# Two transformer blocks on one core: closing an output projection's banks one by one, seven of eight norm operands summed by VectorE, and products of the norm one ahead of the residual sums

## The reference, cut to what matters

```
# first block, layers 0 (gated delta net) and 1 (mLSTM)
hs = hs + keep * rms_norm(mix, norm_w[i, 1])
f = conv_ffn(rms_norm(hs, norm_w[i, 2]), ...)
hs = hs + keep * rms_norm(f, norm_w[i, 3])
# second block, layers 0 (short conv, attention) and 1 (GLA, MLA)
x = layer_norm(ALPHA * x + y, ln_mix_g[layer], ln_mix_b[layer])
x = layer_norm(ALPHA * x + swiglu(...), ln_ffn_g[layer], ln_ffn_b[layer])
```

## Time and profile before

| | |
|---|---|
| median of 3 runs | 1445.23 us (1445.07 to 1447.6) |
| span of the profiled execution | 1443.1 us; the median of the runs is 2.1 us above it, and no other time of that execution is listed |
| TensorE busy | 1423.5 us (99%), 11333 matmuls |
| VectorE busy | 1013.4 us (70%), 1701 instructions |
| ScalarE busy | 779.4 us (54%), 1399 instructions |
| mean granted clock of TensorE | 0.999 of full speed |
| chain that ended last | PE 81%, DVE 12%, issue 3%, ACT 3% |

### The profile page before, as it was taken

The page is one execution under the profiler, slowest core; times in us unless marked ns, Lnnn a source line. Parts: engine busy times, 40 slices in busy tenths (PEclk is TensorE's granted clock), DMA queues, the critical chain, the costliest instruction groups (busy, mean ns, idle before and its releaser), DMA issues.

```text
span 1443.1 us, 31771 instructions
## 1 busy us (share of the span) xinstructions
PE 1423.5 (99%) x11333; PEld 1363.9 (95%) x11333; DVE 1013.4 (70%) x1701; ACT 779.4 (54%) x1399; POOL 294.0 (20%) x348
## 2 busy tenths in 40 slices
PE   9999999999999999999999999999999999999997
PEld 8999888899999999999999999999999989999986
DVE  7884957659876477569888477587664687776645
ACT  6556324556655366466565356464453567654542
POOL 3804002103444000002544000013330012033310
PEclk9999999999999999999999999999999999999999
DMA  7551231244655535344666544546556433565552
GB/s 256 177 175 47 88 101 47 93 142 160 190 175 175 175 119 189 103 146 128 193 189 189 182 134 152 164 146 200 183 168 204 152 116 118 163 217 186 183 180 91
DMA packets 60996, 223.57 MB, mean 155 GB/s; under 512 B 6768, under 2 KB 6896, under 8 KB 60528
## 3 DMA queue, kind: packets, MB, share of 16 engines
q1 hardware_dynamic: 60624, 220.17, 48.1%
q10 hardware_dynamic: 288, 2.23, 0.4%
HBM read 221.32 MB, written 1.05 MB: 154 GB/s over the span
## 4 chain that ended last, share of the span: by engine, by line
PE 81%; DVE 12%; issue 3%; ACT 3%; DVEq 1%; ACTq 0%; POOL 0%; POOLq 0%
PE bank L440 20%; PE bank L441 20%; PE bank L442 20%; DVE wlo L415 3%; PE bank L461 2%; PE bank L1168 2%; PE bank L462 1%; PE bank L468 1%; DVE bank L947 1%; PE bank L3284 1%; PE bank L3285 1%; PE bank L3287 1%; ACT cv L831 1%; DVE cv L839 1%; DVE work L1782 1%
## 5 line engine op out<-in xcount | busy, mean ns | idle before, releaser
L415 DVE TENSOR_TENSOR wlo<-raw,whi 128x1024 fp32r<-128x1024 f32 x397 | 501.4, 1268 | 249.3 <-ACT whi L410 248.8
L410 ACT ACTIVATE whi<-raw 128x1024 fp32r<-128x1024 f32 x397 | 415.1, 1056 | 288.6 <-PE bank L442 240.6
L440 PE MATMUL bank<-xs,whi 128*128 128x258 f32 (+2 forms) x1984 | 569.2, 287 | 0.0
L441 PE MATMUL bank<-xs,whi 128*128 128x258 f32 (+2 forms) x1984 | 563.9, 284 | 0.0
L442 PE MATMUL bank<-xs,wlo 128*128 128x258 f32 (+2 forms) x1984 | 561.6, 283 | 0.0
L440 PEld LDWEIGHTS bank<-xs,whi 128*128 128x128 f32 x1984 | 374.2, 189 | 3.0 <-issue 1.6
L442 PEld LDWEIGHTS bank<-xs,wlo 128*128 128x128 f32 x1984 | 375.0, 189 | 0.0
L441 PEld LDWEIGHTS bank<-xs,whi 128*128 128x128 f32 x1984 | 374.3, 189 | 0.6 <-issue 0.2
L440 PE MATMUL bank<-hf,whi 128*128 (+3 forms) x848 | 241.3, 285 | 2.0 <-DVE cv L839 0.8
L441 PE MATMUL bank<-hf,whi 128*128 (+3 forms) x848 | 240.3, 283 | 0.0
L442 PE MATMUL bank<-hf,wlo 128*128 (+3 forms) x848 | 240.2, 283 | 0.0
(11 more groups left out here) (516 smaller groups left out, 1671.8 us busy)
## 6 DMA issues: line engine op xcount, KB each, us to landing
raw<-stream SPq DMA_DIRECT2D x412, 512.0 KB, 3.7
con<-consts SPq DMA_DIRECT2D x1, 1284.5 KB, 10.5
big<-mla ACTq DMA_DIRECT2D x1, 1152.0 KB, 7.8
hs_sb<-hs SPq DMA_DIRECT2D x2, 544.0 KB, 4.2
work<-last ACTq DMA_DIRECT2D x1, 1024.0 KB, 9.1
y_out<-work SPq DMA_DIRECT2D x4, 256.0 KB, 2.0
par<-params SPq DMA_DIRECT2D x1, 420.0 KB, 7.9
par<-params SPq DMA_DIRECT2D x1, 224.0 KB, 4.8
```

Source lines behind the costliest of these rows:

```text
L410: nc.scalar.activation(whi[:, s, :], raw[:, s, :], ACT.Copy).then_inc(hi_split, 1)
L415: nc.vector.tensor_tensor(wlo[:, s, :], raw[:, s, :], whi[:, s, :].bitcast(F32), ALU.subtract).then_inc(block_split, 1)
L440: nc.tensor.matmul(out_, whi[:, slot, w], hi, start=start, stop=False)
L441: nc.tensor.matmul(out_, whi[:, slot, w], lo, start=False, stop=False)
```

## The change

The last two rows of each output projection in `pe_wide` are taken together: bank by bank, six matmuls each, so that bank m closes 6 matmuls after bank m - 1. The number of matmuls is the same. In `post` joints VectorE adds seven squares, not five, and scales seven banks, sum and scaled copy of a tile taking turns; TensorE sums two operands, not four. The high part of the third block goes from ScalarE to VectorE, behind the scaled copies. Behind the scale, the product of tile m + 1 goes ahead of the residual sum of tile m. In `ln` joints VectorE adds seven tiles, TensorE sums two operands, not six; the third block's high part is made by ScalarE as soon as its slot is free, and its low part in two halves, the first before the mean is subtracted, the second behind the third tile. The loads of ScalarE's table go ahead of the splits of the output projection.

```diff
@@ -455,8 +455,12 @@
                 pe.wait_ge(*S("norm", "act").at(f"{name}_hi{k}"))
                 for j in range(AHEAD):
                     o, s = rhs_out(g0 + j, phase), (b0 + j) % SLOTS
+                    by_half = name.startswith("ln") and j == AHEAD - 1
+                    if k == 0 and by_half:
+                        pe.wait_ge(*S("norm", "dve").at(f"{name}_third"))
+                    if k == (KC // 2 if by_half else 0):
+                        pe.wait_ge(block_split, splits(b0 + j))
                     if k == 0:
-                        pe.wait_ge(block_split, splits(b0 + j))
                         pe.wait_ge(bank_free, g0 + j + 1)
...
+        def last_two():
+
+            pe.wait_ge(block_split, splits(b0 + n - 1))
+            for k in (n - 2, n - 1):
+                ready(pe, k, None)
+            for m in range(8):
+                for k in (n - 2, n - 1):
+                    last = three(rhs_out(g0 + m, phase), (b0 + k) % SLOTS, m, hf[:, half[k], T], hf[:, half[n + k], T], False, k == n - 1)
+                    if m == 7:
+                        last.then_inc(block_used, 1)
+                    elif k == n - 1:
+                        last.then_inc(*S("wide", "pe").mark(f"{phase}_m{m}"))
 
         if n == 22:
             rows(0)
             with pe.Fori(0, 2) as i:
                 for k in range(1, 9):
                     rows(k, i)
-            for k in range(17, 22):
+            for k in range(17, n - 2):
                 rows(k)
+            last_two()
...
-    FIRST_SUM, IN_BANK = 5, 5
+    FIRST_SUM, IN_BANK = 7, 7
...
-        sums_pe(pe, name, post_src(name), g, ((5, True, False), (6, False, False), (0, False, False), (7, False, True)), T1, POST_FIRST[name])
+        sums_pe(pe, name, post_src(name), g, ((0, True, False), (7, False, True)), T1, POST_FIRST[name])
...
-        split_hi(act, used_after(phase) + AHEAD - 1)
         act.wait_ge(*S("norm", "pe").at(name))
...
         def scaled(m):
+            nc.vector.tensor_scalar(y[:, m, lo:T1], bank[(g - 8 + m) % 8][:, lo:T1], pv("norm_w", row * KC + m), None, ALU.mult).then_inc(bank_free, 1)
+
+        for m in range(FIRST_SUM):
             dve.wait_ge(*S("norm", "act").at(f"{name}_{m}"))
-            nc.vector.tensor_scalar(y[:, m, lo:T1], bank[(g - 8 + m) % 8][:, lo:T1], pv("norm_w", row * KC + m), None, ALU.mult).then_inc(bank_free, 1)
-
-        scaled(0)
-        for m in range(1, FIRST_SUM):
-            dve.wait_ge(*S("norm", "act").at(f"{name}_{m}"))
-            if m > 1:
-                dve.wait_ge(*v.at(f"{name}_sum{m - 1}"))
-            nc.vector.tensor_tensor(sq[:, 0, lo:T1], sq[:, 0, lo:T1], sq[:, m, lo:T1], ALU.add).then_inc(*v.mark(f"{name}_sum{m}"))
-        for m in range(1, IN_BANK):
-            scaled(m)
-        split()
+            if m:
+                if m > 1:
+                    dve.wait_ge(*v.at(f"{name}_sum{m - 1}"))
+                nc.vector.tensor_tensor(sq[:, 0, lo:T1], sq[:, 0, lo:T1], sq[:, m, lo:T1], ALU.add).then_inc(*v.mark(f"{name}_sum{m}"))
+            if m < IN_BANK:
+                scaled(m)
+        third_split(dve, phase)
...
+    def third_split(dve, phase):
+
+        n = used_after(phase) + AHEAD - 1
+        s = n % SLOTS
+        dve.wait_ge(hi_split, splits(n - 1))
+        dve.wait_ge(block_loaded[s], 16 * (n // SLOTS + 1))
+        dve.wait_ge(block_used, n - SLOTS + 1)
+        nc.vector.tensor_copy(whi[:, s, :], raw[:, s, :]).then_inc(hi_split, 1)
+        split_lo(dve, n)
...
+    def add_y(dve, name, lo):
+
+        y_step(dve, name, 0)
+        h_step(dve, name, 0)
+        y_step(dve, name, 1)
+        for m in range(1, KC):
+            if m + 1 < KC:
+                y_step(dve, name, m + 1)
+            h_step(dve, name, m)
+            lo(m - 1)
+        lo(KC - 1)
...
-        for m in range(KC):
-            add_y(dve, post, m)
-            if m:
-                lo(m - 1)
-        lo(KC - 1)
+        add_y(dve, post, lo)
...
+        act.wait_ge(hi_split, splits(fourth(phase) - 1))
         split_hi(act, fourth(phase))
...
-    YSUM = 3
+    YSUM = 7
...
-        sums_pe(pe, name + "m", ln_src(name), g, ((0, True, False), (3, False, False), (4, False, False), (5, False, False),
-                                                  (6, False, False), (7, False, True)), T2)
+        sums_pe(pe, name + "m", ln_src(name), g, ((0, True, False), (7, False, True)), T2)
...
-            act.wait_ge(block_used, used_after(PHASE_BEFORE[phase]) - 1)
+            act.wait_ge(block_used, used_after(PHASE_BEFORE[phase]) - 2)
             nc.scalar.activation(xs[:, 0:KC, T2:TB], alone(beta, 2), ACT.Copy).then_inc(*a_.mark(f"{name}_bhi"))
+            split_hi(act, FIRST_BLOCK[phase] + AHEAD - 1)
...
+    def third_low(dve, name, phase, part):
+
+        n = FIRST_BLOCK[phase] + AHEAD - 1
+        s, w = n % SLOTS, slice(part * BLOCK // 2, (part + 1) * BLOCK // 2)
+        dve.wait_ge(hi_split, splits(n))
+        nc.vector.tensor_tensor(wlo[:, s, w], raw[:, s, w], whi[:, s, w].bitcast(F32), ALU.subtract
+                                ).then_inc(*((block_split, 1) if part else S("norm", "dve").mark(f"{name}_third")))
...
-            split()
+            third_low(dve, name, phase, 0)
...
+            if phase and m == 2:
+                third_low(dve, name, phase, 1)
...
         gdn_mix_act(act)
+        nc.scalar.preload_act_table_set(LN_EXP)
         split_all(act, split_hi, "gdn_out", 1, COUNT["gdn_out"] - 2)
-        nc.scalar.preload_act_table_set(LN_EXP)
```

More of the change, by code:

```diff
@@ L538, in rows @@
                     bank_ready(pe, (g0 + m) % 8)
-                last = three(rhs_out(g0 + m, phase), (b0 + k) % SLOTS, m, hf[:, half[at] if i is None else at, T], hf[:, half[lo] if i is None else lo, T], k == 0, k == n - 1)
-                if i is None and k == n - 1 and m < 7:
-                    last.then_inc(*S("wide", "pe").mark(f"{phase}_m{m}"))
+                last = three(rhs_out(g0 + m, phase), (b0 + k) % SLOTS, m, hf[:, half[at] if i is None else at, T], hf[:, half[lo] if i is None else lo, T], k == 0, False)
             if done:
                 last.then_inc(block_used, 1)
+        def last_two():
[9 more added lines that the diff above has]
+                        last.then_inc(*S("wide", "pe").mark(f"{phase}_m{m}"))
         if n == 22:
@@ L558, in pe_wide @@
                         between(pe, k)
-            for k in range(together, n):
+            for k in range(together, n - 2):
                 rows(k)
+            last_two()
     def pe_sum(pe, name, g, src, T):
@@ L734, in add_y, with h_step @@
                                            ).then_inc(*v.mark(f"{name}_y{m}"))
+    def h_step(dve, name, m):
+        v, t = S("norm", "dve"), slice(POST_FIRST[name], T1)
         dve.wait_ge(*v.at(f"{name}_y{m}"))
@@ L821, in last_act @@
             if m == 4:
+                act.wait_ge(hi_split, splits(fourth("ev_in") - 1))
                 split_hi(act, fourth("ev_in"))
@@ L2341, in ln_act, with ln_dve @@
         act_scale(act, name + "v", g + 1, rs[:, 0, 0:T2], T2, D, eps_ln, meanwhile=lambda: split_hi(act, fifth(phase)) if phase == "od_in" else None)
-    def ln_dve(dve, n, which, layer, phase, wide, split):
+    def third_low(dve, name, phase, part):
[4 more added lines that the diff above has]
+                                ).then_inc(*((block_split, 1) if part else S("norm", "dve").mark(f"{name}_third")))
+    def ln_dve(dve, n, which, layer, phase, wide):
         name, g = f"ln{n}", G[f"lm{n}"]
@@ L3410, in _ @@
         even_act(act)
-        split_all(act, split_hi, "ev_out", 1)
         nc.scalar.preload_act_table_set(LN_EXP)
+        split_all(act, split_hi, "ev_out", 1, COUNT["ev_out"] - 2)
         ln_act(act, 0, "ln_mix", 0, 'up2')
@@ L3422, in _ @@
         odd_act(act)
-        split_all(act, split_hi, "od_out", 1)
         nc.scalar.preload_act_table_set(LN_EXP)
+        split_all(act, split_hi, "od_out", 1, COUNT["od_out"] - 2)
         ln_act(act, 2, "ln_mix", 1, 'up3')
```

24 lines of the change are left out of this document (12 added, 12 removed).

## The result

The change makes the kernel a little slower: 1448.39 us median of 15 runs (1446.82 to 1451.89) against 1445.23 of 15 runs of before (1444.79 to 1447.82). The ratio of the runs is 1.0018, 95% interval 1.0010 to 1.0025, so the loss is real. It lies at the edge of what the prediction counted as no change: by the ratio it is 0.18%, by the medians 3.2 us (0.22%), where the prediction drew the line at 2.9 us, 1448.1. The forecast was 1445.9 us, range 1442.5 to 1451. The profiled execution of after took 1448.75 us, with a span of 1446.8 (before 1443.1).

A forecast was written before the change was run, and what follows sets the result against it. TensorE, busy 99%, leaves gains only at seven joints, where VectorE's chain sets the sums. Post -0.85 and ln +1.5 make +0.65 us, added to the 1445.23 median: about 1445.9 us, range 1442.5 to 1451.

The forecast's parts named there:

- VectorE keeps up: Rival: VectorE follows the banks as they close, post and ln joints get shorter by 8.7 us in all, 1436.5; 10%.
- the lost order with the slow cast: Rival: new order in post waves saves nothing (1448.4 us), or the third block's cast runs at its slow bound (1447.5); 12%.
- Post joints, predicted -0.85: Four RMS norm joints: first product 0.38 us later, waves 0.70 shorter; -0.3, -0.3, -0.25 and 0, together -0.85 us.
- half of the wave's gain: Fourth post joint: its step was already near TensorE's own, so half of 0.70 us was taken, giving 0.
- `ln` joints, predicted +1.5: Three layer norm joints: sums wait for VectorE's sum of seven, first centred row 0.5 us later each, +1.5 us together.
- lies beside it: ln waves: the second half of the low part, 0.6 us behind row 2, runs beside TensorE's pace and costs nothing.
- wide range: The forecast's 8-in-10 range for the time, 1442.5 to 1451 us, including the slow bounds and foot of the clock case.
- my own case: Main forecast: post joints -0.85, ln joints +1.5, sum +0.65 us, about 1445.9, own range 1444.5 to 1447.5; 60%.
- signs of being wrong: In the profile: no idle gaps before the sums, granted clock under 1.00 at a joint, or wave steps staying at 1.24.
- the rival that was given 14%: Clock falls in TensorE's new idle gaps before the sums: 1453 us if only in ln, near 1460 in all joints; 14%.
- my gaps are shorter: TensorE's gaps before the sums, 1.4 us (post) and 2.2 (ln), are shorter than the 2.7 after which the clock fell.
- Table loads at nothing: ScalarE's table loads (1.28 us) moved ahead of the splits hide in its idle time: nothing, at most 0.6 us each.

The follow-up runs named there:

- experiment 2: Kernel before with one part alone, products one ahead of the residual sums in the four post waves: 1442.67 us, ratio 0.9981.
- after again: The kernel after, unchanged, timed and profiled a second time: 1448.81 us, ratio to before 1.0017.
- Kernels 1, 5, 6 and 10: Kernel after with filling matmuls in all seven gaps (1445.10 us), three ln gaps (1445.18), four post gaps (1447.75), seven per ln gap (1445.38).
- kernel 5: Kernel after with 15 filling matmuls in each of the three ln gaps, post gaps left open: 1445.18 us, ratio to before 0.9994.
- experiment 12: Kernel after with all seven gaps filled by matmuls, and table loads put back behind the splits: 1447.17 us, ratio to before 1.0013.
- experiment 4: Kernel before with one part alone, the projections' banks closed over the last two rows: 1449.70 us, ratio 1.0020.

## Why the prediction was right or wrong

*What it got right.* That VectorE's chain, not the closing of the banks, sets the sums: start at T + 1.27 (`post`, predicted 1.37) and 2.11 (`ln`, predicted 2.2); first product 0.28 later (0.38), first centred row 0.48 later (0.5). The cast takes 0.68 us (0.69, an estimate from an operation of half its length). The wave's step is 1.12 (1.13), and experiment 2 shows that gain alone. So the rival "VectorE keeps up" is out, and so is the lost order with the slow cast.

*Post joints, predicted -0.85, measured -1.74.* Sizes: from first product to the end of the wave the first joint is 0.75 shorter where 0.70 was counted, and the later start costs 0.1 less; that makes -0.5 instead of -0.3 or -0.25 in three joints. In the fourth I took half of the wave's gain and got -0.22 instead of 0; experiment 2 puts that joint's gain at 0.49.

*`ln` joints, predicted +1.5, measured +2.0 without the clock.* The first and third are +0.56 as said. The second is +0.91, since the step "lies beside it" for the half low part fails there: this joint's wave also carries pair sums. Its wave takes 10.0 us instead of 9.6 in before. VectorE is busy 9.30 of 10.00 us in it, and it gives the pace:

```profile
1137.78 0.69 DVE L2382 TENSOR_TENSOR wlo<-raw,whi 128x512 fp32r<-128x512 f32 x1
1138.38 0.42 DVE L784 TENSOR_TENSOR sq<-sq 128x256 f32<-128x256 f32 x1
1138.71 0.42 DVE L2416 SCALAR_TENSOR_TENSOR y<-bank,y 128x256 f32<-128x256 f32 x1
```

(VectorE, timeline of after again.) I had read the earlier trace rows of the first `ln` joint and taken them for three.

*The sum* of these is +0.3, less than the +0.65 predicted, so by this count the time would have been 1445.5. That it comes so near is partly luck: the `post` joints are 0.9 better than counted and the `ln` joints 0.5 worse.

*The clock.* The time lies in the wide range (1442.5 to 1451) but outside that of my own case (1444.5 to 1447.5), and one of the signs of being wrong that I had named is there, a granted clock under 1.00 at a joint. So the time of 1448.4 is not explained by my case; it needs the rival that was given 14%: the clock does fall, in the `ln` joints only, at gaps of 2.1 us. The step that failed is "my gaps are shorter". The earlier trace rows showed one fall, behind 2.7 us of idling, and I took that for the bound; here 2.1 us were enough. The rival's price was wrong too. I had it at 2.5 us in each of three joints (1453); a fall costs 0.8 to 1.1 us, and each of the three profiles has one in one of its three joints. That 1448.4 lies in the wide range at all comes of a range that reached from my case to the foot of this one, and of no sum in the forecast.

The Trainium skill ("TensorE: Matmul & The Clock Gate", section "Why this matters for your kernels") warns of idle gaps between bursts of matmuls, of longer ones than these. Kernels 1, 5, 6 and 10 bear the warning out in the middle of a program and show it for a gap of 2.1 us already: filling the three is worth 3.2 us of median here.

*Table loads at nothing.* That holds only together with the rest: without the moves the changed kernel is 2.1 us slower (experiment 12), and the two closing rows alone, without this and the other parts around them, lengthen the joints by 2.05 us (experiment 4). I had read each edit against the kernel before and not against the other edits.

*Open.* One fall costs about 1 us, while the medians differ by 3.2 (after against kernel 5). The least times of after and after again lie 1.8 and 1.5 above that of kernel 5, one fall and a few tenths; but 14 of their 26 runs lie at 1448.39 and higher. These 14 have mean clocks of 0.993 to 0.996, the other 12 of 0.996 to 0.998, so they spent more time at half clock, in several falls. A second or third fall at a joint or the one at 119 us would do this; which, and whether the change makes the one at 119 us more frequent, isn't shown.

## What to carry to other kernels

Handing sums from TensorE to a VectorE that is the later of the two turns TensorE's work into idle time. Let the waiting engine do its share of operands up to the moment at which the other is done: six and two, four and four were better here than seven and one (no other split was run). A gap of some 2 us in TensorE's stream can cost more than its length, because the clock can fall behind it; if it can't be closed, matmuls of no use in it were worth their place here. And put an independent operation (0.12 us a row here) between a VectorE operation and the one that uses its result.

## What the runs showed of the hardware that I had not expected

- The granted clock fell right behind an idle gap of 2.1 us, stayed near 0.5 for about 3.4 us although TensorE was busy throughout (3.40 of 3.40 us), and came back. In each of three profiles it happened at one of three equal gaps, at the first joint in one and at the second in two. Behind gaps of 1.1 to 1.4 us no profile shows it.
- It also fell where no such gap stands: at 119 us TensorE is busy 1.20 of 1.20 us just ahead, with small matmuls, and the only idle time to speak of ahead of that is one of some 0.57 us at 116 us, which all fourteen profiles have. The clock was 0.50 in six of them, from somewhere between 118.7 and 120.4 us on, for 3.4 us in two and for 6.8 us in four, and 1.00 in the others, at the same code. By the times it costs up to 2.6 us.
- Interleaving two rows frees their weight slots together: no matmul was added, and by itself it made each `ln` joint 0.95 to 0.97 us longer (experiment 4).
